# First projection of a two-layer decoder trunk: the rotary half swap by fp32 products on TensorE

## The reference

```python
h = rms_norm(x, g_pre) * (1.0 + scale) + shift
gq, gk, gv, gz, glr, rq, rk, rv, rz = jnp.split(h @ w_in, offsets, axis=-1)
log_a = log_sigmoid(glr @ w_gate_up + b_gate) / GLA_TAU
x1, x2 = x[..., :half], x[..., half:]          # rotary, for rq and rk, half = 32
rotary = concatenate([x1 * cos - x2 * sin, x2 * cos + x1 * sin])
```

## Time and profile before

| | us |
|---|---|
| median of 3 runs | 2617.9 (2617.62 to 2619.27) |
| the profiled execution | 2623.62 |
| its span, first to last instruction | 2621.8 |
| TensorE busy in the span | 2447.8 (93%) |
| VectorE, ScalarE, POOL busy | 1350.0, 917.0, 788.4 |
| the input projection of layer 0 (with its preparation) | about 0 to 625 |

### The profile page before, as it was taken

One profiled execution on the slowest core, in us unless ns is written; L12 is line 12 of the kernel. 1 busy time (PEld: TensorE's weight loads), 2 busy tenths in 40 slices (PEclk: granted clock), 3 DMA queues, 4 the chain that ended last, 5 costly groups with the idle time before them and its releaser, 6 DMA issues. The chain is left out here.

```text
span 2621.8 us, 53672 instructions
## 1 busy us (share of the span) xinstructions
PE 2447.8 (93%) x20947; PEld 1485.1 (57%) x21012; DVE 1350.0 (51%) x2947; ACT 917.0 (35%) x2644; POOL 788.4 (30%) x849
## 2 busy tenths in 40 slices
PE   6989999997999977999999999967999999999998
PEld 2434444444566533444444444446787887878876
DVE  3422222122687745983625626326566675666656
ACT  3633232322111114442322322135454554544541
POOL 2540000021111103550000000007456465565554
PEclk9989999998999987999999999988999999999998
DMA  8541212134544554551111121125322231221303
GB/s 295 153 137 48 89 46 79 43 122 134 210 152 159 157 176 117 170 160 46 71 66 53 61 82 49 57 73 164 96 83 89 66 106 58 82 90 58 99 30 93
DMA packets 254520, 270.12 MB, mean 103 GB/s; under 512 B 30263, under 2 KB 188023, under 8 KB 254314
## 3 DMA queue, kind: packets, MB, share of 16 engines
q1 hardware_dynamic: 187962, 219.66, 25.5%
q10 hardware_dynamic: 66352, 47.51, 6.5%
HBM read 179.76 MB, written 87.36 MB: 102 GB/s over the span
## 5 line engine op out<-in xcount | busy, mean ns | idle before, releaser
L624 PE MATMUL inc_b<-raw_next,inc_w_hi 128*128 128x512 f16 (+1 forms) x760 | 228.6, 382 | 3.2 <-POOL inc_w_lo L573 2.0
L624 PE MATMUL inc_b<-keep,inc_w_hi 128*128 128x512 bf16 (+1 forms) x762 | 227.1, 379 | 1.4 <-ACT inc_ub L2063 0.2
L624 PE MATMUL inab_b<-inab_wt,keep 128*128 128x512 f16 x768 | 168.0, 381 | 1.6 <-POOL inab_wt L573 1.6
L624 PE MATMUL inab_b<-inab_wt,raw_next 128*128 128x512 f16 x768 | 166.4, 379 | 0.0
L1169 PE MATMUL mixab_y<-keep,mixab_oT_hi 128*128 128x512 f16 x512 | 153.3, 381 | 7.6 <-DVE mixab_f_y L1249 5.9
L2157 DVE SCALAR_TENSOR_TENSOR inc_acc<-inc_ub,inc_taps,inc_acc 128x512 f32<-128x512 f32 x192 | 152.1, 792 | 6.8
L2063 ACT ACTIVATE inc_ub<-inc_b 128x512 f32<-128x512 f32 x96 | 57.0, 594 | 251.5 <-PE inc_b L624 247.3
L2153 DVE COPY inc_ub<-inc_halo 128x3 f32<-128x3 f32 x96 | 24.6, 256 | 231.8 <-ACT inc_ub L2063 231.8
L624 PE MATMUL inc_b<-raw_next,inc_w_lo 128*128 128x512 bf16 x368 | 140.5, 382 | 0.0
L624 PE MATMUL inc_b<-keep,inc_w_lo 128*128 128x512 bf16 x366 | 138.7, 379 | 0.0
L912 ACT ACTIVATE inab_vz<-inab_b 128x512 f32<-128x512 f32 x66 | 39.4, 597 | 253.8 <-PE inab_b L624 235.0
(11 more groups left out here) (578 smaller groups left out, 6128.5 us busy)
## 6 DMA issues: line engine op xcount, KB each, us to landing
tmp_qkv<-stage_next SPq DMA_DIRECT2D x98, 256.0 KB, 2.0
stage_next<-in_w_in_c ACTq DMA_DIRECT2D x30, 512.0 KB, 4.5
inab_stage<-in_w_in_ab ACTq DMA_DIRECT2D x24, 512.0 KB, 4.1
raw_next<-tmp_qkv SPq DMA_DIRECT2D x8, 1536.0 KB, 8.1
mixc_qkv<-tmp_qkv SPq DMA_DIRECT2D x8, 1536.0 KB, 7.7
inab_wt<-in_w_ada SPq DMA_DIRECT2D x10, 1024.0 KB, 14.8
keep<-in_x_prompt SPq DMA_DIRECT2D x16, 512.0 KB, 4.1
tmp_v<-inab_vz SPq DMA_DIRECT2D x32, 256.0 KB, 3.7
```

Of the source, the lines that this page charges most:

```text
L624: last = nc.tensor.matmul(dst, lhs(a, k), rhs(b, k), start=(k == 0 and i == 0), stop=(k == KT - 1 and i == len(PASSES) - 1))
```

## The change

The exchange of the halves moves from VectorE to TensorE. Groups 11 to 14 are now used: each multiplies one quarter of the columns of `r` (128 x 512, fp32) by a permutation table `swap`, and ScalarE copies the result into `rs` once `u_done` has come. TensorE starts them when group 10 has been copied out. VectorE's rotary chain starts when group 14 is out (in the sample block, where the order is 0 to 10, 15, 11 to 14, 16, likewise) and has no copies. The turns of the second to fourth tile's squares, modulations and roundings are set anew, each weight unit has a group of its own (none at 5, 6, 11, 12, 13), and the gate group's quarters take chunks 0 to 3 first and then 4 to 7, where before they took the even ones and then the odd ones.

```diff
+    t = {"ident": np.eye(P, dtype=f), "swap": np.eye(P, dtype=f)[i ^ 32]}
-    RING, G = 4, 11 + 4 * TPB
+    RING, G = 4, 15 + 4 * TPB
-        return (*range(11), *range(15, 15 + (4 * TPB if n == BLK else 2)))
+        return range(G) if n == BLK else (*range(11), 15, *range(11, 15), 16)
     TURN = (4, 10, 18, 24)
-    SQUARE, LOW, HI = (1, 7, 15, 20), (5, 15, 19, 25), (8, 17, 22, 28)
-    HI_S = 16
+    SQUARE, LOW, HI = (1, 7, 13, 19), (5, 11, 19, 25), (8, 14, 22, 28)
+    HI_S = 14
-    slots = [g for g in order(BLK) for _ in range(2 if g in (2, 8) else 1) if not 5 <= g < 7]
-    unit_at = {g: [AHEAD + i for i, s in enumerate(slots) if s == g] for g in slots}
+    unit_at = {g: AHEAD + i for i, g in enumerate(g for g in range(G) if not (5 <= g < 7 or 11 <= g < 14))}
 # ScalarE
+                elif g < 15:
+                    act.wait_ge(u_done, b + 1)
+                    act.activation(rs[:, g - 11, 0:n], src[:, 0:n], ACT.Copy).then_inc(evac, 1)
 # VectorE
-            dve.wait_ge(evac, RING + b * G + 11)
-            dve.wait_ge(u_done, b + 1)
-            for part in range(4):
-                other = part ^ 1
-                last = dve.tensor_copy(rs[part * 32:(part + 1) * 32, :, 0:n], r[other * 32:(other + 1) * 32, :, 0:n])
-            chain.link(last)
+            dve.wait_ge(evac, RING + b * G + (15 if n == BLK else 16))
 # TensorE
-                            k = 2 * part + odd
+                            k = part + 4 * odd
+                elif g < 15:
+                    if g == 11:
+                        pe.wait_ge(evac, RING + b * G + 11)
+                    last = nc.tensor.matmul(dst[:, 0:n], tv["swap"], r[:, g - 11, 0:n], start=True, stop=True)
```

More of the change, by code:

```diff
@@ L43 @@
 LEVELS = (2, 4, 8, 16, 32)
-TABLE_ORDER = ("reset", "reset_s", "dec", "dec_s", "retd", "retd_s", "sel", "sel_s", "ident", "neg", "neg_s", "seq", "eye_h",
+TABLE_ORDER = ("swap", "reset", "reset_s", "dec", "dec_s", "retd", "retd_s", "sel", "sel_s", "ident", "neg", "neg_s", "seq", "eye_h",
                *(f"pick{w}" for w in (1, *LEVELS)), "incl", "incl_s")
@@ L641, in phase_in_ab @@
     nb, nt = seq // BLK, seq // P
-    names = ["reset", "reset_s", "dec", "dec_s", "retd", "retd_s"]
+    names = ["swap", "reset", "reset_s", "dec", "dec_s", "retd", "retd_s"]
     tab = ph.sb("tab", [P, width(names)])
@@ L711, in phase_in_ab @@
     GATES = {1: (0, 1), 3: (2, 3)}
-    def order(n):
-        return (*range(11), *range(15, 15 + (4 * TPB if n == BLK else 2)))
-    TURN = (4, 10, 18, 24)
-    SQUARE, LOW, HI = (1, 7, 15, 20), (5, 15, 19, 25), (8, 17, 22, 28)
-    HI_S = 16
-    AHEAD = TPB
-    slots = [g for g in order(BLK) for _ in range(2 if g in (2, 8) else 1) if not 5 <= g < 7]
-    unit_at = {g: [AHEAD + i for i, s in enumerate(slots) if s == g] for g in slots}
+    TURN = (4, 10, 18, 24)
+    SQUARE, LOW, HI = (1, 7, 13, 19), (5, 11, 19, 25), (8, 14, 22, 28)
+    HI_S = 14
+    AHEAD = TPB
+    unit_at = {g: AHEAD + i for i, g in enumerate(g for g in range(G) if not (5 <= g < 7 or 11 <= g < 14))}
+    def order(n):
+        return range(G) if n == BLK else (*range(11), 15, *range(11, 15), 16)
     def chan(g):
@@ L786, in outputs @@
                 for j in range(2):
-                    sp.wait_ge(evac, RING + b * G + 12 + j)
+                    sp.wait_ge(evac, RING + b * G + (12, 17)[j])
                     for half in range(2):
@@ L796, in outputs @@
                 i, tc = divmod(j, tiles)
-                sp.wait_ge(evac, RING + b * G + 11 + j + 1)
+                sp.wait_ge(evac, RING + b * G + 15 + j + 1)
                 dst = io["v0" if i < 2 else "z0"]
@@ L841, in _ @@
             weights.lo(pool, u)
-        for g in order(BLK):
+        for g in range(G):
             for tc in range(TPB):
@@ L848, in _ @@
                     prep.split_lo(pool, TPB + tc, tc * P, P, prep.at(1))
-            for i in unit_at.get(g, ()):
-                weights.lo(pool, i)
+            if g in unit_at:
+                weights.lo(pool, unit_at[g])
         for b in range(1, nb - 1):
@@ L939, in groups @@
                         prep.split_hi(act, t, t + 1 if rows == P else nt, tc * P, rows, prep.at(b + 1))
-                if first:
-                    for i in unit_at.get(g, ()):
-                        weights.hi(act, i)
+                if first and g in unit_at:
+                    weights.hi(act, unit_at[g])
                 if first and g in GATES:
@@ L955, in _ @@
         rows_out.load(act, 0)
-        groups(nb - 1, BLK, [(nt, NS)], rows_at={**dict(zip(range(16, 30, 2), range(7))), 30: 7})
+        groups(nb - 1, BLK, [(nt, NS)], rows_at={**dict(zip(range(16, G - 1, 2), range(7))), G - 1: 7})
         groups(nb, NS, [])
@@ L982, in work @@
         def work(b, n, next_tiles):
-            chain.turn(5 * b if n == BLK else 5 * b + 1)
+            chain.turn(4 * b if n == BLK else 4 * b + 1)
             def nx(tc):
@@ L1041, in work @@
                 high(tc)
-            chain.close(6 if len(next_tiles) == 1 else 5)
+            chain.close(5 if len(next_tiles) == 1 else 4)
         with dve.Fori(0, nb - 1) as b:
```

1 line of the change is left out of this document (removed).

## The result

| | us | ratio to before |
|---|---|---|
| before, first comparison, 6 runs | 2617.76 (2615.30 to 2624.61) | |
| after, first comparison, 6 runs | 2628.86 (2628.52 to 2630.55) | 1.0036 [1.0025, 1.0048] |
| before, with two later comparisons, 56 runs | 2621.98 | |
| after, with the same, 28 runs | 2628.54 | 1.0025 [1.0017, 1.0030] |

The change makes the kernel slower, by 11.1 us in the first comparison and by 6.6 us in all runs together (the interval of the last row is a bootstrap of the two medians). The forecast was +5.7 us. The interval of all runs is +4.4 to +8.0 us. Single executions of one kernel have a standard deviation of 2.9 us (before) and 2.7 us (after), so the median of six says little about 5 us; the phase, read from the traces, says more.

What follows compares the result with a forecast made beforehand. TensorE's matmuls bound blocks 1 to 3; block 0 had a stall. Added 13.1 us less 7.4 returned gives +5.7 on 2617.9: 2623.6 us, own range 2621.4 to 2626.4 (chance 0.55), 8-in-10 range 2618.5 to 2629.5.

Steps and rivals of the forecast that it cites:

- the rival with late weights: Block 0: weights late throughout, only 0 to 3.5 us returned, kernel at 2627.5 to 2631 us; chance 0.15.
- the return of block 0: Block 0: 6.8 us from group 19 starting earlier, plus 1.0 clock, less 0.4 at group 27: 7.4 us (2 to 12).
- The price of the products: Swaps on TensorE: four fp32 products at 0.86 us each, as at L1104, 3.44 us per block.
- The rival of cheap products: Swaps: at most 0.52 us per 512 columns, as fp32 transposes; with full return 2614 to 2616 us; chance 0.03.
- Blocks 1 and 2: TensorE there: the products plus 0.35 us for restart and type change, 3.8 us a block (3.4 to 4.5).
- Block 3: No transposes cover group 10's eviction, so the swap starts about 0.9 us late: 4.4 us added (3.4 to 5.0).
- the sample block: Four swap products on 64 columns, behind group 15, which hides the wait: 1.1 us added (1.0 to 1.3).
- The chain in block 0: Steps: group 15 at 116.5, rotary passes from 119.3, normalisation's end at 138.1, group 19 at 140.3 instead of 147.06.
- What is late next: Block 0, after the stall: unit 24, with a modulation ahead of it, makes group 27 about 0.4 us late.
- The clock: Block 0: TensorE's slow clock after the old stall cost 2.1 us, 0.9 counted elsewhere; 1.0 us more taken back.
- The order of chunks: Gate group: both orders wait for chunk 7, so 0 (1 us gained to 0.4 us lost).
- the full return: Block 0 gives back 10 to 12 us, units 12 and 16 being ready: 2619 to 2621 us; chance 0.27.

## Why the prediction was right, and where not

The mechanism was right: products paid in blocks 1 to 3, a stall of block 0 given back in part. The forecast of +5.7 us stands between the phase's +5.0 us in the traces and the +6.6 us of the pooled medians. The forecast time does less well: 2623.6 us against 2628.86, which lies outside the forecast's own 2621.4 to 2626.4 and 0.6 us inside the wide range. The term that was off is the base, 2617.9 us: the median of the 56 runs of before is 4 us higher, and with it the sum gives 2627.7 us. The number of the rival with late weights (2627.5 to 2631) fits the first comparison better, though what it describes did not happen. And the sum owes something to luck, since its errors offset each other: the added work was put 1.4 us too high, the return of block 0 some 0.5 us too high, and inside that return a chain that came earlier than forecast paid for a wait that was not foreseen. Point by point:

- *The price of the products* (3.44 us a block): right, 3.43 to 3.44 us by doubling them. The rival of cheap products falls; even four of 8 columns take 1.03 us with their tail. Its price came from the fp32 transposes; their instructions start 0.11 us apart, and so do those of the 8-column products, so that row says little of a rate per column.
- *Blocks 1 and 2* (+3.8 us each, 3.4 to 4.5): the step was right, a term was missing. Products and restart cost 3.58 us, so the restart is 0.14 us where 0.35 was allowed without a row to show it; the old kernel lost 0.56 us at the third tile, and the new turns gave it back: +3.0 us. That is under the 3.5 that was to show the forecast right, and just above the 3 that was to show it wrong. The row of block 1 in the earlier trace rows had 0.66 us of idle time, which I read as nothing; 0.35 of it is that wait.
- *Block 3* (+4.4) and *the sample block* (+1.1): +4.45 and +1.26. The wait for group 10 is 0.78 us where 0.9 was taken.
- *The chain in block 0*: to within 1.5 us at each step by the traces' own times. Group 15 at 116.93 (forecast 116.5), rotary at 119.10 (119.3), normalisation's end at 136.60 (138.1), group 19 at 139.25 (140.3). Counted from the second tile's transposes, which come 0.6 us later here, group 19 comes 8.4 us earlier than before; the forecast was 6.8. Unit 16 is what it waits for, 0.56 us.
- *What is late next* (0.4 us before group 27): mis-sized, and at another place. Group 27 is 0.3 us late, but group 23 waits 1.5 to 2.35 us for unit 20, by the held v buffer. I had written that SP's v stores come earlier and had not followed the fifth eviction to them, though the old trace shows its wait of 12.27 us. This ate the clock's 1.0 us and more.
- *Block 0's return* (7.4 us, 2 to 12): 6.7 us as the mean of three traces, 6.9 on one footing. One reason for the spread of the three is TensorE's clock at the start of group 1, which rises latest in the first trace.
- *The clock*: right. The stretch before block 1 has a granted clock of 0.98 where the earlier trace rows has 0.95, since no long stall is left: from 66 us on it is 1.00.
- *The order of chunks* (0): from VectorE's last chunk to group 1's first record the old order takes 2.05 us in two traces, the new one 1.91 in two and 1.52 in the first. The first trace has the record that the others lack; on one footing the gain is 0.14 us, nearly nothing.

The rivals: weights late all through block 0 did not come, though each weight wait is of that kind; the full return did not come because of units 12, 16 and 20. What the profile of before could have told and I did not ask: what VectorE's late start alone is worth. I had ScalarE's hold of group 9's eviction in the chain of the change and did not price its end by itself; a spread of the units takes the stall from 11.91 to 1.41 us without a product on the bound. No run joins the swap with that spread: it could still remove the waits for units in block 0, but not what blocks 1 to 3 pay.

## What to carry to other kernels

Work moved from an idle engine to the one that bounds the program is paid wherever that bound holds: here three blocks and the samples pay 11.7 us for a stall that only the first block had. Ask first why the stalled chain started late; a helper task that shares an evicting engine's queue may hold it, and moving that task puts nothing on the engine that bounds the program. After a stall goes, follow every buffer behind it to the next wait.

## What the runs showed of the hardware that was not expected

- Four fp32 products of 128x128 weights take 3.67 us on 512 columns and still 1.03 us on 8, both with their tail: far from proportional to columns. What sets the lower time no run shows.
- One-input VectorE instructions are held by POOL too. The normalisation of 128x1024 took 0.74 us alone and 2.65 us in the kernel with the moved normalisation and spread units, where a POOL subtraction of 2.13 us began 0.03 us ahead of it:

```profile
123.06 2.13 POOL L573 TENSOR_TENSOR inab_wt<-inab_stage,inab_wt 128x1024 f16<-128x1024 f32 x1
123.09 2.65 DVE L409 TENSOR_SCALAR keep<-keep,inab_rstd 128x1024 f32<-128x1024 f32 x1 [1.11 <-POOL inab_rstd L404]
```

  The Trainium skill (SBUF — State Buffer, Who interferes with whom) says that a copy or tensor_scalar can enter a mode that takes the shared ports, and that the one to issue second is blocked for the whole of the first instruction. The row roughly agrees: 2.65 us is 0.2 us under 2.13 - 0.03 + 0.74 = 2.84 us. Which mode the instruction was in no run here shows.
- Small POOL operations pay as well: the mean square and the power on 128x1 took 0.19 and 0.55 us alone, 2.21 and 2.48 us beside VectorE's rotary passes (121.26 and 123.47 above) in the kernel with the units spread alone:

```profile
121.38 2.21 POOL L402 TENSOR_SCALAR inab_meansq<-inab_sumsq 128x1 f32<-128x1 f32 x1 [5.03 <-ACT keep L375]
123.68 2.48 POOL L404 TENSOR_TENSOR inab_rstd<-inab_meansq,inab_mhalf 128x1 f32<-128x1 f32 x1
```

- Two short waits of TensorE close together went with the lower clock level, where two of the same sum, but apart, were not. With the units spread alone, waits of 1.41 and 1.50 us around the third transposes go with a granted clock of 0.50 from 136.6 to 143.5, and the six groups behind take 2.85 us longer; in the kernel after, waits of 0.56 and 2.35 us, some 21 us apart, leave it at 1.00.
